# New RWKV states of the samples accumulated in PSUM in the layout of the outputs

## The chip, the cores and the metric

The kernel runs on one core of one Trainium2 chip. The metric is the device time of one execution in microseconds (us). Before the change the median of three runs is 1883.43 us (1877.42 to 1886.05). The profile is of one further execution, which took 1890.77 us; from its first to its last instruction it spans 1888.9 us.

## The reference, cut to what matters

The reference is one step of a two-layer decoder trunk: an even layer with MLA attention and RWKV-7 heads side by side, and an odd layer with gated linear attention and eight experts. Only the RWKV state of the even layer matters here:

```python
def rwkv7_scan(r, w, k, v, a, b, S0):
    def step(S, inp):
        rt, wt, kt, vt, at, bt = inp
        sa = jnp.einsum('bhvk,bhk->bhv', S, at)
        S = S * wt[:, :, None, :] + sa[..., None] * bt[:, :, None, :] + vt[..., None] * kt[:, :, None, :]
        return S, jnp.einsum('bhvk,bhk->bhv', S, rt)
```

A state S is a matrix [value, key] of 64 x 64 for each of the 8 heads. The prompt (256 tokens) starts from zero. The 8 samples of 8 tokens start from `state_rwkv` and hand back `new_rwkv_sample` of shape [sample, head, value, key], 1 MB in all. After a sample's 8 tokens, the new state is S0 decayed by the product of its eight w, plus the sum over the eight tokens of u b and v k, where u is the matrix product with the state (`sa`) and each b and k is decayed from its token to the end. All is fp32.

## The kernel before, in words

Every engine has its own program, written out by hand in blocks; the engines meet only in semaphores, and in a barrier at the end of a block. `next_part()` (L152) is two barriers with a clearing of semaphores between them. Nothing reorders the work: its order is the order of the lines.

The RWKV part lies between two calls of `next_part()` (L1150, L1779) and has three blocks.

**Block 1** makes r, w, k, v, a and b of all 320 tokens, with the channels on the partitions (four groups of 128 channels, two heads each). At its end the state S0 of each sample is turned by TensorE into S0T (key on the partitions, L1382, taken by ScalarE at L1321), and b and k are turned into rows with the tokens on the partitions: rowB and rowK, each of two tiles of 128 prompt tokens and one of the 64 sample tokens (L1393; taken in turn by VectorE, L1280, and ScalarE, L1325). rowV is made in the same way earlier (L1356, L1307). `wends` is the decay of each sample over its eight tokens (L1272).

**Block 2** inverts small triangular matrices per chunk of 64 tokens.

**Block 3** (L1494 to L1776) runs over the prompt's four chunks of 64 tokens. On TensorE `own_terms` and `transitions` make each chunk's terms, `step(c)` (L1560) carries the state on, `from_state(c)` (L1567) gives the outputs y. On VectorE `taken` takes the transitions (its last instruction, L1662, frees TensorE for the own terms of chunks 2 and 3), `advance(c)` (L1671, L1673) adds and decays the state, `y_add(c)` adds y. The samples' u comes at L1623 and is copied to U2. Their new states are made so: for each head VectorE spreads u and v over the samples (`spread`: ub and vb, L1683, L1684, each u or v times the 0/1 mask `bsel`), TensorE multiplies with the rows of b and of k (`new_states`, L1577, L1578: keys on the partitions, [sample, value] in 512 columns of one bank), VectorE adds S0T and multiplies with `wends` (`new_state`, L1689, L1690). Only two banks and two ub/vb buffers take turns. The result has keys on the partitions and the output wants values there: so TensorE turns the prompt's state and the eight samples' states (L1654, nine times four transposes), ScalarE and VectorE copy them in turn (L1767, L1741), and SP issues nine stores of 128 KB each (L1774, whose line in the profile is the helper's, L241). SP then waits for all of them, and block and part end.

The next part begins with four loads of 1 MB (L1895, `ring`) and with TensorE's L1918; none of it starts before the barrier. ScalarE's last work of block 3 ahead of the copies is `hT` (L1761, L1762), behind a wait for the y of all chunks.

Of the kernel before, what the change touches and what calls it, by code (L numbers as in the profile page):

```python
# [10 lines left out]
ALU = mybir.AluOpType  # L11
# [4 lines left out]
P = 128  # L16
# [42 lines left out]
def constants():  # L59
# [43 lines left out]
    bsel[:64] = (i[:64] // DS == np.arange(NB)[None, :])  # L103
# [36 lines left out]
def model(nc, A, O):  # L140
# [22 lines left out]
    with ctx:  # L163
# [243 lines left out]
        with ExitStack() as ev:  # L407
# [744 lines left out]
            with ExitStack() as rk:  # L1152
# [11 lines left out]
                with ExitStack() as st:  # L1164
# [12 lines left out]
                    rn = sbuf(st, "kk_norm", [P, 3, RH])  # L1177
                    rx = dif[:, :, :].rearrange("p c t -> p (c t)")[:, 0:3 * RDIM].rearrange("p (i h d) -> p i h d", i=3, h=RH)
# [3 lines left out]
                     kk_full, kk_var, kk_root, rn_ready, rx_ready, bc_full, kk_ready, ex_in, ex_out, bo_ready, bo_full, b_ready, k_ready, bonus_ready,  # L1182
# [3 lines left out]
                         "norm_full", "kk_ready", "exp_in", "exp_out", "bonus_in", "bonus_sum", "b_ready", "k_ready", "bonus_ready",  # L1186
                         "v_turned", "v_taken", "rows_turned", "rows_act", "rows_dve"))
                    kk, rT, kT, vT = t1, rwT[:, 0:4, :], rwT[:, 4:8, :], rwT[:, 8:12, :]
                    with nc.Block() as block:
# [14 lines left out]
                        def _(v):  # L1204
# [67 lines left out]
                            dv(v, v.tensor_copy(wends[:, :, :], bonus[:, :, SEQ + DS - 1:TOK:DS]))  # L1272
                            v.wait_ge(bo_full, 1)
# [3 lines left out]
                            for n in range(0, 6, 2):  # L1277
                                v.wait_ge(row_full, n + 1)
                                r = TILES[n % 3][1]
                                v.tensor_copy((rowB, rowK)[n // 3][0:r, n % 3, :], ps[n % 4][0:r, :]).then_inc(row_dve, 1)  # L1280
# [3 lines left out]
                        def _(s):  # L1284
# [37 lines left out]
                            for n in range(1, 6, 2):  # L1322
                                s.wait_ge(row_full, n + 1)
                                r = TILES[n % 3][1]
                                s.activation((rowB, rowK)[n // 3][0:r, n % 3, :], ps[n % 4][0:r, :], ACT.Copy).then_inc(row_act, 1)  # L1325

                        @block.tensor
                        def _(t):
# [25 lines left out]
                            for i, (lo, r) in enumerate(TILES):  # L1354
                                for c in range(4):
                                    mm = t.transpose(ps[5 + i][0:r, c * P:(c + 1) * P], vT[:, c, lo:lo + r], C("ident"))  # L1356
                                mm.then_inc(v_full, 1)
# [26 lines left out]
                            for n in range(6):  # L1384
                                lo, r = TILES[n % 3]
                                if n < 4:
                                    t.wait_ge(st_free, n + 5)
                                else:
                                    t.wait_ge(row_act if n % 2 else row_dve, n // 2 - 1)
                                for c in range(4):  # L1390
                                    if n % 3 == 0:
                                        t.wait_ge(b_ready if n < 3 else k_ready, c + 1)
                                    mm = t.transpose(ps[n % 4][0:r, c * P:(c + 1) * P], (bF, kF)[n // 3][:, c, lo:lo + r], C("ident"))  # L1393
# [96 lines left out]
                with ExitStack() as st:  # L1490
# [8 lines left out]
                    U2 = sbuf(st, "U2", [64, RDIM])  # L1499
                    ub = sbuf(st, "ub", [64, 2, NB, RD])  # L1500
                    vb = sbuf(st, "vb", [64, 2, NB, RD])
                    SN = S0T
                    NR = 8
                    OB = (4, 6, 2, 3)
                    srow2 = rwT[0:RD, :, :].rearrange("p c t -> p (c t)")[:, 0:NR * RDIM].rearrange("p (n k) -> p n k", n=NR)
                    yv = mixT[:, 4:8, :]
                    row_out = [Signal(sem(f"row_out{n}")) for n in range(NR)]
                    (a_full, a_ready, r_full, r_ready, w_full, wu_act, wu_dve, p_full, p_ready, q_full, q_dve, q_act, s_full, s_sum, s_ready,
                     y_full, y_added, sy_full, sy_ready, tr_full, mv_full, rhs_copied, r2_ready, u2_full, u2_ready, y2_full, y2_ready, blk_ready, n_full,
                     n_ready, o_full, o_act, o_dve) = (sem(x) for x in (  # L1510
                         "a_turned", "a_ready", "mv_first", "mv_ready", "w_full", "w_act", "w_dve", "p_full", "p_ready", "q_full", "q_dve", "q_act",
                         "s_full", "s_sum", "s_ready", "y_full", "y_added", "sy_full", "sy_ready", "sy_turned", "mv_full", "rhs_copied", "rhs2_ready", "u2_full",
                         "u2_ready", "y2_full", "y2_ready", "blk_ready", "new_full", "new_ready", "row_full", "row_act", "row_dve"))
# [11 lines left out]
                    with nc.Block() as block:  # L1525
                        @block.tensor
                        def _(t):
# [42 lines left out]
                            def new_states(hs_):  # L1570
                                for h in hs_:
                                    h0, pr = 64 * (h % 2), h // 2
                                    t.wait_ge(blk_ready, h + 1)
                                    if h % 2 == 0 and pr >= 2:
                                        t.wait_ge(n_ready, pr - 1)
                                    out = ps[pr % 2][h0:h0 + 64, :]
                                    t.matmul(out, rowB[0:64, 2, h * RD:(h + 1) * RD], ub[:, h % 2, :, :].rearrange("p b v -> p (b v)"), start=True, stop=False)  # L1577
# [1484 lines left out]
```

## Time and profile before

| | us |
|---|---|
| median of the runs | 1883.43 |
| profiled execution, and its span | 1890.77, 1888.9 |
| TensorE busy | 1790.3 |
| VectorE busy | 666.3 |
| ScalarE busy | 353.5 |
| mean granted clock, share of the full one | 0.962 |

The busy times are of the whole kernel, whose larger part is the experts' layer. The part that is changed is read from the timelines: a row of a timeline has the start, the length from the first start to the last end, engine, line, operation, output and inputs with their shapes, and the count; in brackets stands how long the engine sat idle before it and who let it go. Matmuls are shown with modelled ends, so that pitches are taken from starts. A plain fp32 matmul shows as two matmul records, a transpose as one.

### The profile page before, as it was taken

How to read it: one execution, taken by the hardware profiler on the slowest of the kernel's cores; microseconds unless marked ns; L12 is line 12 of the kernel's file. 1: busy time of each engine (PE TensorE's matmuls, PEld its weight loads, DVE VectorE, ACT ScalarE, POOL GpSimd, SP SyncE). 2: the span in 40 equal slices, each digit the busy share in tenths (PEclk: the TensorE clock that was granted, in tenths of full speed). 3: DMA queues.
4: the chain of work that ended last, by engine and by line, in shares of the span. 5: the costliest groups of instructions: out<-in, count | busy, mean ns of one | idle time of the engine just before them, and what ended most of it. 6: DMA issues, size and time to landing. Idle time of an engine off the chain costs nothing.

```text
span 1888.9 us, 42360 instructions
## 1 busy us (share of the span) xinstructions
PE 1790.3 (95%) x19238; PEld 1148.9 (61%) x19238; DVE 666.3 (35%) x1243; ACT 353.5 (19%) x584; POOL 29.7 (2%) x37
## 2 busy tenths in 40 slices
PE   7989898689799999998999999999999999999997
PEld 6957564587599999996833535344353443535344
DVE  4534332774675554656642110121102111120121
ACT  3223231501243332444310000000000000000002
POOL 0010000000000000000000000000000000000000
PEclk9989998698799999999989999999999999999998
DMA  9130540200654444425499999999999999997994
GB/s 289 45 109 1 150 142 11 37 3 2 181 155 142 150 145 126 155 68 150 143 379 416 417 412 417 397 382 417 364 417 373 405 409 366 417 354 290 399 416 159
DMA packets 166440, 463.28 MB, mean 245 GB/s; under 512 B 27770, under 2 KB 110876, under 8 KB 135412
## 3 DMA queue, kind: packets, MB, share of 16 engines
q1 hardware_dynamic: 164910, 457.37, 65.2%
q8 instruction: 151, 2.47, 0.5%
q0 software_dynamic: 1152, 3.15, 0.4%
q14 instruction: 29, 0.24, 0.0%
q10 hardware_dynamic: 198, 0.05, 0.0%
HBM read 451.57 MB, written 8.95 MB: 244 GB/s over the span
## 4 chain that ended last, share of the span: by engine, by line
PE 52%; DVE 1%; ACT 0%; issue 0%; DVEq 0%; ACTq 0%
PE bank L2623 46%; PE bank L2591 1%; PE bank L310 1%; PE bank L312 1%; PE bank L311 1%; PE bank L2554 0%; PE bank L2475 0%; PE bank L2597 0%; PE bank L2561 0%; PE bank L2490 0%; PE bank L2509 0%; PE bank L2482 0%; ACT ring L2787 0%; DVE mixT L2805 0%; PE bank L2494 0%; PE bank L2686 0%
## 5 line engine op out<-in xcount | busy, mean ns | idle before, releaser
L2623 PE MATMUL bank<-ring,x 128*32 128x512 f32 (+1 forms) x6144 | 587.5, 540 | 0.0
L2623 PEld LDWEIGHTS bank<-ring,x 128*32 128x32 f32 x6144 | 195.0, 110 | 359.9 <-issue 357.2
L2623 PE MATMUL bank<-ring,hid 128*32 128x256 f32 x5376 | 291.5, 379 | 0.0
L2623 PEld LDWEIGHTS bank<-ring,hid 128*32 128x32 f32 x5376 | 174.7, 110 | 117.1 <-issue 3.1
L310 PE MATMUL bank<-x_hi,w_hi 128*128 128x320 f32 (+1 forms) x488 | 151.8, 311 | 0.0
L312 PE MATMUL bank<-x_hi,w_lo 128*128 128x320 f32 (+1 forms) x488 | 150.8, 309 | 0.0
L311 PE MATMUL bank<-x_lo,w_hi 128*128 128x320 f32 (+1 forms) x488 | 150.8, 309 | 0.0
L2129 DVE TENSOR_TENSOR w_lo<-ring,w_hi 128x2048 fp32r<-128x2048 f32 (+2 forms) x51 | 112.5, 2208 | 96.2 <-ACT w_hi L2053 95.9
L2987 DVE TENSOR_TENSOR hrow<-sil,bank 128x512 f32<-128x512 f32 (+1 forms) x48 | 26.9, 616 | 296.1 <-PE bank L2623 296.1
L2950 DVE TENSOR_TENSOR xT<-xT,bank 128x320 f32<-128x320 f32 x56 | 23.5, 483 | 277.4 <-PE bank L2591 277.4
L2053 ACT ACTIVATE w_hi<-ring 128x2048 fp32r<-128x2048 f32 (+2 forms) x51 | 94.1, 1846 | 128.9 <-PE bank L312 124.3
L2769 ACT ACTIVATE sil<-bank 128x512 f32<-128x512 f32 (+1 forms) x48 | 22.6, 544 | 478.9 <-PE bank L2623 478.9
L310 PEld LDWEIGHTS bank<-x_hi,w_hi 128*128 128x128 f32 (+1 forms) x488 | 90.9, 186 | 1.9 <-issue 1.0
L311 PEld LDWEIGHTS bank<-x_lo,w_hi 128*128 128x128 f32 (+1 forms) x488 | 90.9, 186 | 0.6 <-issue 0.2
L312 PEld LDWEIGHTS bank<-x_hi,w_lo 128*128 128x128 f32 (+1 forms) x488 | 90.9, 186 | 0.4
L2776 ACT ACTIVATE Y<-bank 128x256 f32<-128x256 f32 x24 | 7.5, 384 | 403.8 <-PE bank L2623 403.8
L310 PE MATMUL bank<-hid,w_hi 128*128 128x320 f32 x240 | 75.2, 313 | 4.1 <-DVE w_lo L2129 4.1
L311 PE MATMUL bank<-hid,w_hi 128*128 128x320 f32 x240 | 74.8, 312 | 0.0
L312 PE MATMUL bank<-hid,w_lo 128*128 128x320 f32 x240 | 74.8, 312 | 0.0
L2969 DVE COPY listed<-bank 32x2 f32<-32x2 f32 x108 | 16.5, 153 | 145.9 <-PE bank L2597 144.5
L310 PE MATMUL bank<-proj_x_hi,proj_w_hi 128*128 128x320 f32 (+1 forms) x160 | 51.2, 320 | 6.5 <-DVE proj_w_lo L587 6.5
L311 PE MATMUL bank<-proj_x_lo,proj_w_hi 128*128 128x320 f32 (+1 forms) x160 | 50.5, 316 | 0.0
(569 smaller groups left out, 2209.7 us busy)
## 6 DMA issues: line engine op xcount, KB each, us to landing
ring<-in_moe_w_gu SPq DMA_DIRECT2D x128, 1024.0 KB, 15.9
ring<-in_moe_w_down SPq DMA_DIRECT2D x112, 1024.0 KB, 13.1
ring<-in_moe_w_gu SPq DMA_DIRECT2D x128, 768.0 KB, 10.7
ring<-in_ffn_w_gu_even SPq DMA_DIRECT2D x44, 512.0 KB, 4.9
pages<-in_cache_mla SPq DMA_DIRECT2D x128, 144.0 KB, 2.4
ring<-in_w_in_odd SPq DMA_DIRECT2D x12, 1024.0 KB, 5.6
ring<-in_ffn_w_down_even SPq DMA_DIRECT2D x10, 1024.0 KB, 5.1
proj_ring<-in_w_in_even SPq DMA_DIRECT2D x9, 1024.0 KB, 8.0
```

The source lines that it names most:

```text
L310: t.matmul(out, w_hi, x_hi, start=start, stop=False)
L311: t.matmul(out, w_hi, x_lo, start=False, stop=False)
L312: return t.matmul(out, w_lo, x_hi, start=False, stop=stop)
L2053: s.activation(whi[:, i % NSP, 0:size(i)], ring[:, i % NS, 0:size(i)], ACT.Copy).then_inc(hi_ready, 1)
L2129: v.tensor_tensor(wlo[:, i % NSP, 0:size(i)], ring[:, i % NS, 0:size(i)], whi[:, i % NSP, 0:size(i)].bitcast(F32), ALU.subtract).then_inc( ...
L2591: mm = t.matmul(ps[banks[y]][:, 0:TOK], Y[part, s_, z * P:(z + 1) * P], selT[part, s_, :], start=(s_ == 0), stop=(s_ == SG - 1), tile_posi ...
L2623: mm = t.matmul(ps[banks[g3]][SL * y:SL * y + SL, 0:w], act[:, g3, k, :], m_ring[:, slot, at + y * w:at + (y + 1) * w], start=start, stop= ...
L2769: ins = s.activation(sil[:, s_, 0:quarter(g)], ps[s_][:, 0:quarter(g)], ACT.Silu)
L2776: s.activation(Y[:, s_, :], ps[bank][:, 0:256], ACT.Copy).then_inc(y_ready, 1)
L2950: last = v.tensor_tensor(xT[:, 2 * y + z, :], xT[:, 2 * y + z, :], ps[bank][:, 0:TOK], ALU.add)
L2969: last = v.tensor_copy(listed[SL * y:SL * y + SL, s_, :], ps[6][SL * s_:SL * s_ + SL, 0:2])
L2987: ins = v.tensor_tensor(hrow[:, 512 * s_:512 * s_ + n], sil[:, s_, 0:n], ps[3 + s_][:, 0:n], ALU.mult)
```

## The change

It has these parts.

- Block 1, VectorE: eight small multiplications make `bks`, the samples' columns of b and of k times `wends` of their sample (each 128 x 64).
- Block 1, TensorE and the copies: the rows are five banks of 512 columns, no longer six: b and k of the two prompt tiles (banks 0 to 3), and bank 4 with the samples' decayed b in partitions 0 to 63 and their decayed k in partitions 64 to 127, by eight matmuls with the identity in two column tiles. rowB[:, 2] gets bank 4 whole. Bank 4 waits for `bonus_ready` and `bks_ready`. The samples' v is also written to partitions 64 to 127 (four matmuls with the identity, one more copy of ScalarE, to rowK).
- Block 3, VectorE: the mask `bsel` has 128 rows. `spread(h)` makes BKb, the rows of b and k of head h times the mask, one instruction of 128 x 512. Four stand at the block's start, four after the L1703 of before; between L1703 and these, four instructions of 128 x 512 multiply S0T with `wends` in place. U2 is written into rowK, below v.
- Block 3, TensorE: the new `new_states(pr)` has, for each sample and each of two heads, one matmul of the decayed S0T with the identity and one of [u; v] with BKb, accumulated at 64 partitions x 64 columns: 32 matmuls a pair of heads, values on the partitions, in four banks of their own. The order is step 2, from_state 2, states of pair 0, step 3, states of pair 1, from_state 3, pairs 2 and 3.
- The end: four copies of 128 x 512 (VectorE pairs 0 and 2, ScalarE 1 and 3, behind `hT`), four stores of 256 KB, and one turn, copy and store of 128 KB for the prompt. The 32 transposes of samples' states go, with their copies.

```diff
+                            v.wait_ge(k_ready, 4)
+                            for n, src in enumerate((bF, kF)):
+                                for c in range(4):
+                                    last = v.tensor_tensor(bks[:, n, c, :]..., src[:, c, SEQ:TOK]..., wends[:, c, :]...to_broadcast([P, NB, DS]), ALU.mult)
+                            last.then_inc(bks_ready, 1)
...
+                                if i == 2:
+                                    s.activation(rowK[64:128, 2, :], ps[7][64:128, :], ACT.Copy)
...
+                                    if i == 2:
+                                        t.matmul(ps[7][64:128, cols], vT[:, c, lo:lo + r], C("ident"), start=True, stop=True, tile_position=(0, 64))
...
+                                        for q in range(2):
+                                            mm = t.matmul(ps[4][64 * q:64 * q + 64, cols], bks[:, q, c, :], C("ident"), start=True, stop=True, tile_position=(0, 64 * q))
...
-                            def new_states(hs_):
-                                for h in hs_:
-                                    t.wait_ge(blk_ready, h + 1)
-                                    t.matmul(out, rowB[0:64, 2, h * RD:(h + 1) * RD], ub[:, h % 2, :, :]..., start=True, stop=False)
-                                    mm = t.matmul(out, rowK[0:64, 2, h * RD:(h + 1) * RD], vb[:, h % 2, :, :]..., start=False, stop=True)
+                            def new_states(pr):
+                                for b in range(NB):
+                                    for h in (2 * pr, 2 * pr + 1):
+                                        hs, _, _ = head(h)
+                                        t.matmul(ps[N_BANK[pr]][hs, b * RD:(b + 1) * RD], S0T[:, b, pr, :], C("ident")[:, hs], start=True, stop=False, tile_position=(0, hs.start))
+                                        mm = t.matmul(ps[N_BANK[pr]][hs, b * RD:(b + 1) * RD], UV2[:, h * RD:(h + 1) * RD], BKb[:, h, b, :], start=False, stop=True,
+                                                      tile_position=(0, hs.start))
+                                mm.then_inc(n_full, 1)
...
-                            for n in range(1 + NB):
-                                for pr in range(4):
-                                    src = ST[:, NCH, pr, :] if n == 0 else SN[:, n - 1, pr, :]
-                                    mm = t.transpose(ps[OB[n % 4]][0:RD, pr * P:(pr + 1) * P], src, C("ident"))
+                            for pr in range(4):
+                                mm = t.transpose(ps[5][0:RD, pr * P:(pr + 1) * P], ST[:, NCH, pr, :], C("ident"))
...
+                            for pr in range(4):
+                                last = v.tensor_tensor(S0T[:, :, pr, :], S0T[:, :, pr, :], wends[:, pr, :]...to_broadcast([P, NB, RD]), ALU.mult)
+                            last.then_inc(s0_ready, 1)
+                            for h in range(4, RH):
+                                last = spread(h)
+                            last.then_inc(blk_ready, 1)
...
+                            for pr in (1, 3):
+                                s.wait_ge(n_full, pr + 1)
+                                s.activation(news[:, pr, :, :]..., ps[N_BANK[pr]][:, :], ACT.Copy).then_inc(n_act, 1)
...
+                            for pr in range(4):
+                                sp.wait_ge(n_act if pr % 2 else n_dve, pr // 2 + 1)
+                                store(sp, O["new_rwkv_sample"][0, :, 2 * pr:2 * pr + 2].rearrange("b h v k -> (h v) b k"), news[:, pr, :, :])
+                            sp.wait_ge(o_act, 1)
+                            store(sp, O["new_rwkv_prompt"][0, 0].rearrange("h v k -> v h k"), srow2.rearrange("v (h k) -> v h k", h=RH))
```

## Rows read from the trace of the kernel before

**Rows 1.** The profile's page, part 1: busy time, share, instructions.

```profile
PE 1790.3 (95%) x19238; PEld 1148.9 (61%) x19238; DVE 666.3 (35%) x1243; ACT 353.5 (19%) x584; POOL 29.7 (2%) x37
```

**Rows 2.** Timeline of TensorE, the end of block 3 and the next part.

```profile
458.36 0.66 PE L1567 MATMUL bank<-hT,ST 64*64 64x64 f32 x16
...
480.73 5.92 PE L1654 MATMUL bank<-consts,S0T 128*64 128x128 f32 x32
492.85 4.61 PE L1918 MATMUL bank<-mixT,consts 128*128 128x320 f32 x8 [6.20 <-PEq L157]
```

**Rows 3.** Timeline of SP: the sample stores, and the next part's loads.

```profile
482.54 6.08 SPq L241 DMA_DIRECT2D out_new_rwkv_sample<-rwT  x8
492.80 5.34 SPq L1895 DMA_DIRECT2D ring<-in_w_out_even  x4
```

**Rows 4.** Stretches: length; busy of PE, PEld, DVE, ACT, POOL; granted clock, DMA share, GB/s.

```profile
335.00:345.00 10.00, 3.22 (x21) 2.90 (x21) 7.74 (x19) 6.35 (x13) 0.00 (x0) 0.50 0.94 146
430.00:440.00 10.00, 10.00 (x130) 10.00 (x129) 0.00 (x0) 1.18 (x2) 0.00 (x0) 0.54 0.01 2
460.00:465.00 5.00, 4.83 (x44) 2.05 (x42) 4.93 (x11) 1.82 (x4) 0.00 (x0) 1.00 0.02 5
470.00:475.00 5.00, 5.00 (x10) 1.25 (x8) 4.15 (x8) 0.00 (x0) 0.00 (x0) 0.50 0.00 0
482.00:483.00 1.00, 1.00 (x7) 0.84 (x5) 0.51 (x1) 0.32 (x1) 0.00 (x0) 0.50 0.08 13
490.00:491.00 1.00, 0.00 (x0) 0.00 (x0) 0.00 (x0) 0.00 (x0) 0.00 (x0) 0.50 0.65 95
```

**Rows 5.** Timeline of VectorE in block 1.

```profile
362.80 1.68 DVE L1257 TENSOR_TENSOR t<-t,bank 128x320 f32<-128x320 f32 x4
...
372.48 1.68 DVE L1275 TENSOR_TENSOR bonus<-bank,rwT 128x320 f32<-128x320 f32 x4
...
375.51 0.69 DVE L1280 COPY rowK<-bank 128x512 f32<-128x512 f32 x1 [0.16 <-PE bank L1393]
```

**Rows 6.** Timeline of ScalarE, the end of block 1.

```profile
375.95 0.59 ACT L1325 ACTIVATE rowK<-bank 64x512 f32<-64x512 f32 x1 [2.72 <-PE bank L1393]
```

**Rows 7.** Timeline of TensorE in block 1, and block 2's start.

```profile
355.16 2.82 PE L1356 MATMUL bank<-consts,rwT 128*128 128x128 f32 x12
...
376.84 1.56 PE L1419 MATMUL bank<-hT,bF 64*64 64x128 f32 x24 [0.93 <-PEq L1189]
```

**Rows 8.** Timeline of VectorE in block 3.

```profile
444.88 0.67 DVE L1703 TENSOR_TENSOR rhs<-rhs,bank 64x512 f32<-64x512 f32 x1
449.03 0.42 DVE L1705 TENSOR_TENSOR ST<-bank,wend 128x256 f32<-128x256 f32 x1 [3.48 <-PE bank L1553]
...
450.31 0.41 DVE L1662 TENSOR_TENSOR hT<-bank,hT 128x256 f32<-128x256 f32 x1
...
465.78 0.69 DVE L1690 TENSOR_TENSOR S0T<-S0T,wends 128x512 f32<-128x512 f32 x1
466.39 0.41 DVE L1677 TENSOR_TENSOR mixT<-mixT,bank 128x256 f32<-128x256 f32 x1
```

**Rows 9.** One line (L1623): min/median/max ns, first and last start.

```profile
L1623 PE MATMUL bank<-rhs,XT x16: 218/218/218, 450.5 to 451.4; 64*64 64x64 f32 x16
```

**Rows 10.** Timeline of TensorE, two matmul groups with 128 x 64 weights and 64 columns.

```profile
126.41 1.15 PE L828 MATMUL bank<-qpT,consts 128*64 128x64 f32 x16
...
329.17 1.15 PE L1066 MATMUL bank<-mixT,uv 128*64 128x64 f32 x32 [0.58 <-DVE mixT L1107]
```

**Rows 11.** Timeline of TensorE's weight loads where the tile shape changes.

```profile
441.70 0.36 PEld L1612 LDWEIGHTS bank<-consts,SY 128*64 128x64 f32 x4 [0.17 <-issue]
442.26 0.85 PEld L1606 LDWEIGHTS bank<-AV,XT 64*64 64x64 f32 x16 [0.20 <-issue]
```

**Rows 12.** Timeline of ScalarE in block 3.

```profile
463.18 1.92 ACT L1761 ACTIVATE hT<-bonus,vecs 128x320 f32<-128x320 f32 x4 [6.09 <-PE bank L1567]
465.00 1.25 ACT L1762 ACTIVATE hT<-gT 128x1280 f32<-128x1280 f32 x1
```

More of the change, by code:

```diff
@@ L1276, in _ @@
                             last.then_inc(bonus_ready, 1)
-                            for n in range(0, 6, 2):
+                            for n in (0, 2, 4):
                                 v.wait_ge(row_full, n + 1)
-                                r = TILES[n % 3][1]
-                                v.tensor_copy((rowB, rowK)[n // 3][0:r, n % 3, :], ps[n % 4][0:r, :]).then_inc(row_dve, 1)
+                                v.tensor_copy(ROWS[n], ps[n][:, :]).then_inc(row_dve, 1)
                             v.wait_ge(bonus_ready, 1)
@@ L1383, in _ @@
                                 mm.then_inc(st_full, 1)
[L1384 to L1389, printed above, removed]
[L1390 to L1393 removed]
+                            for n in range(5):
+                                t.wait_ge(*((st_free, n + 5) if n < 4 else (bonus_ready, 1)))
+                                if n == 4:
+                                    t.wait_ge(bks_ready, 1)
+                                for c in range(4):
+                                    cols = slice(c * P, (c + 1) * P)
+                                    if n < 4:
+                                        src, lo = (bF, kF)[n // 2], TILES[n % 2][0]
+                                        if n % 2 == 0:
+                                            t.wait_ge(b_ready if n < 2 else k_ready, c + 1)
+                                        mm = t.transpose(ps[n][:, cols], src[:, c, lo:lo + P], C("ident"))
+                                    else:
+                                        for q in range(2):
+                                            mm = t.matmul(ps[4][64 * q:64 * q + 64, cols], bks[:, q, c, :], C("ident"), start=True, stop=True, tile_position=(0, 64 * q))
                                 mm.then_inc(row_full, 1)
@@ L1568, in from_state @@
                                 mm.then_inc(y_full, 1)
-                            def new_states(hs_):
-                                for h in hs_:
-                                    h0, pr = 64 * (h % 2), h // 2
-                                    t.wait_ge(blk_ready, h + 1)
[L1574 to L1577, printed above, removed]
-                                    mm = t.matmul(out, rowK[0:64, 2, h * RD:(h + 1) * RD], vb[:, h % 2, :, :].rearrange("p b v -> p (b v)"), start=False, stop=True)
-                                    mm.then_inc(n_full, 1)
+                            def new_states(pr):
[6 more added lines that the diff above has]
+                                mm.then_inc(n_full, 1)
                             for i in range(2):
```

109 lines of the change are left out of this document (44 added, 65 removed).

## The prediction

> **What bounds the kernel now.** I read the page first: TensorE is busy for 95% of the span [rows 1], but the change touches one stage of some 120 us, so the share says little and the stage has to be read by itself. Then the timelines of its engines from 355 to 500 us, and the stretches with clock and DMA share. The reader is to see three things. First, the part ends in a tail that no other work covers: the transposes of the samples' states start at 480.73 and last 5.92 us [rows 2], the eight sample stores are issued from 482.54 to 488.62 [rows 3], and TensorE then stands still until 492.85, where "PEq L157" says that it was the barrier of the part that held it [rows 2]. Nothing of the next part starts earlier, not even its loads (SP, 492.80 [rows 3]). So whatever moves this barrier moves the whole rest of the kernel by as much. Second, the tail ends with the DMA engines and not with SP: their share is 0.08 in 482 to 483 and 0.65 in 490 to 491 [rows 4], with full slices between; I read 7.7 us of all engines for nine stores of 128 KB, which is 0.85 us a store, against a pitch of 0.68 at which SP issued them. Packets begin at about 482.9 and end at about 490.65, and from there to TensorE's restart are 2.2 us. Third, ahead of the tail the new states are a chain of VectorE and TensorE in turn, and TensorE's clock is lost in it: granted 1.00 (2.4 GHz) in 460 to 465, 0.50 (1.2 GHz) in 470 to 475, where ten matmul records of 512 columns fill 5 us [rows 4].
>
> **Block 1, what is added and what goes.** At its end VectorE gets eight products of 128 x 64. The trace has none of that size; by VectorE's rows of 256 and 512 columns (pitches 0.33 and 0.61 us, the second from the starts 465.78 and 466.39 [rows 8]) a column costs 1.1 ns over a base of 0.06 us, so 64 columns come to 0.13 us and eight to 1.0 us. They stand ahead of L1275, which ran from 372.48 for 1.68 us [rows 5] and now ends near 375.2. The first two copies of rows follow to 376.4. Bank 4 needs `bonus_ready`, at 375.2: eight matmuls with 128 columns, 16 records over two column tiles, 0.9 us if the tiles overlap, 1.7 us if not or at half the clock. Its copy starts at about 376.5 and ends at 377.2. Before, the last to end was ScalarE at 375.95 + 0.59 = 376.54 [rows 6], with VectorE's at 376.20 [rows 5], and TensorE's next block began at 376.84 [rows 7]. So block 1 ends 0.7 us later (0.3 to 1.6).
>
> Further ahead, four matmuls for the second v are eight records of 128 columns behind the twelve of L1356, which took 2.82 us, 0.22 us each [rows 7]: at most 1.8 us for TensorE, and one copy of 0.6 us for ScalarE, behind which stand its copy of the norms, the exponentials and the copies of g. What covers it is VectorE: it is busy without a gap and takes the first result of this chain at 362.80 [rows 5], and by my reading of ScalarE's timeline the exponentials come 3 us ahead of their use. The cover is just enough for the norm, with some tenths left; I count 0, and 1.2 us at worst.
>
> **Block 3, the eight new products on VectorE.** The first four (128 x 512, pitch 0.61, 2.4 us) stand in front of two copies whose readers come ten microseconds later; VectorE was idle there. Cost nothing. The other eight (four decays, four spreads) go between L1703, over at 445.5, and L1705, which started at 449.03 after 3.48 us of idleness [rows 8]. 8 x 0.61 = 4.9 us, so that L1705 starts at 450.4, 1.3 us late. Who waits for that: TensorE's own terms of chunks 2 and 3 stand behind L1662, which ended at 450.72 [rows 8]; one wait of 0.18 us ahead of it goes, so it ends at 451.8. But TensorE was busy with L1623 until its last start at 451.4 [rows 9]. The delay that gets through is 0.4 us.
>
> **Block 3, the chain of states.** From there everything is 0.4 us late until from_state(2), whose 16 records started at 458.36 [rows 2]: it now ends near 459.4. Before, VectorE did four spreads ahead of advance(2), which then started at 460.77; these go, and advance(2) runs at 459.0, as soon as step(2) is done. Now the new matmuls: 128 x 64 weights, 64 columns, 32 to a pair of heads. Two rows bound them. L1066 has just this shape with its column tiles taken in turn: 32 records (16 matmuls) in 1.15 us, less the 0.22 us length of the last, a pitch of 30 ns a record, 60 ns a matmul. L828 has the same shape and stays in one column tile: 16 records in 1.15 us, 62 ns a record, 124 ns a matmul [rows 10]. The new order is two matmuls in one tile, then two in the other, which lies nearer to the first. I take 60 ns: 32 x 60 = 1.9 us a pair (4.0 at the other end). So, with d for a pair and a change of tile shape (64 x 64 to 128 x 64 or back) at 0.2 us as between L1606 and L1612 [rows 11], five of them in all: pair 0 from 459.4 to 461.3, step(3) to 462.2, pair 1 to 464.2, from_state(3) to 465.1, pairs 2 and 3 to 469.0. In letters, from_state(3) ends at 461.3 + 2d and the last pair at 461.4 + 4d.
>
> The Trainium skill ("TensorEngine Tiling (Array Packing)", section Tiling Modes) says that a change of tiling mode, unlike a change of tile, drains TensorE. That speaks against this order, which puts three blocks of one mode between blocks of the other. The trace agrees as to the sign, with 0.17 and 0.20 us of idle weight loads; the rule gives no other price.
>
> **The end.** ScalarE stands behind from_state(3) with `hT`, 463.18 to 466.25, 3.1 us [rows 12], and copies pair 1 after it: 465.1 + 3.1 + 0.7, so that the second sample store is issued at 469.0. (The first, of pair 0, leaves at about 464 and is out of the way.) Pair 3 is copied at 469.8, the prompt's state at 470.5. SP needs 1.33 us to issue a load of 1 MB cut into 1024 pieces (four in 5.34 us) and 0.65 to 0.76 for a store of 512 pieces [rows 3]; a new store has 1024 pieces of 256 B, so I take 1.33: issues at 469.0, 470.3, 471.7 and 473.0. The pieces are as long as before, so that the DMA engines need for the three of 256 KB and the one of 128 KB 7 x 0.85 = 6.0 us. Begun 1.2 us after the issue, they end at 476.2, later than the last issue by enough. Plus the 2.2 us of the barrier: TensorE restarts at 478.4 and not at 492.85. In letters, 474.6 + 2d by this road and 468.2 + 4d by way of the last pair, which takes over above d = 3.2 us.
>
> **The sum.** 492.85 - 478.4 = 14.4 us won, 0.7 us lost in block 1: 13.7 us. The last 0.2 I give for the order within a pair, which is not quite L1066's. 13.5 us off the profiled execution is 1890.8 - 13.5 = 1877.3 us. That execution is 7.3 us over the median of the runs, which is noise and no part of the change; against the median the forecast is 1883.4 - 13.5 = 1869.9 us. All that stands after the barrier, the experts above all, is as before.
>
> **Rivals.**
>
> A. The tiles don't overlap, or the clock stays at 1.2 GHz (either gives about 120 ns a matmul). For it: in the old chain the clock fell [rows 4], and in 430 to 440 it was 0.54 although TensorE was busy all the time, with matmuls of 16 columns [rows 4]. Against it: the old chain was full of gaps, which the new lacks, and 460 to 465, with the 64-column matmuls of step(3) and from_state(3) in it, had 1.00 [rows 4]. d = 4.0: restart at 484.2, won 8.7, less 0.7: 8.0 us, 1875.4 us.
>
> B. The stores from 128 partitions go faster than those from 64. The loads of 1 MB, which have 1 KB pieces, show that the engines can do more. Then SP's issues bound: last issue 473.0 + 1.3 + 0.4 + 2.2 = 476.9, and the win is 15.2 us: 1868.2 us. Against it: in 335 to 345, mostly the loads of the old states in pieces of 256 B, the share was 0.94 at 146 GB/s [rows 4], the stores' rate.
>
> C. Block 1 gives more back: the second v goes through with 1.2 us and bank 4 with 1.6, both at 1.2 GHz. Win 11.5 us, 1871.9 us.
>
> D, the other side: both halves of A together, 240 ns a matmul, d = 7.7 us. The restart is at 468.2 + 30.8 = 499.0 plus 0.7, 6.9 us late: 1890.3 us, slower. It decides from d = 6.0 us, 187 ns a matmul. For it speaks only that both halves have a row; against it what was said under A, and that the tile order isn't that of L828.
>
> E. What VectorE now does ahead of L1705 holds more than one reader, or the new waits (s0_ready, blk_ready) come last: they are posted at 450.4, nine microseconds ahead of their use. I give this no time of its own.
>
> **Chances.** Forecast, between 12 and 15 us won: 0.58. A 0.16, B 0.08, C 0.12, D 0.03, none of these 0.03. A measurement of this kernel can tell about 0.5%, 9.4 us, from no change. The forecast and B lie beyond that, C mostly, A just inside; with the spread of the runs that gives 0.75 for faster, 0.21 for the same, 0.04 for slower. The range for 8 in 10 goes from 1864 (B and 4 us of spread) to 1878 us (A and some spread).
>
> **What would show it.** Right: no L1654 for the samples; records of the new matmuls at 30 ns pitch, a pair in 1.9 us; granted clock near 1.00 in 460 to 470 of the old count; L1705 some 1.3 us later, the own terms 0.4; the DMA share full for about 6 us, and L1918 at about 479, counted from the same start. Block 2's first matmul at 377.5. Wrong: pairs of 4 us with starts 60 ns apart, a clock at 0.50 there, a DMA tail that is longer than 7 x 0.85 us, or a restart that is set by something other than the store of the last states. The forecast falls if L1918 comes after 484, or if the time behind it differs by more than 2 us.

## The result and the profile after

The changed kernel takes 1874.28 us (median of 20 runs, 1863.34 to 1884.31), the kernel before 1886.65 us (20 runs, 1876.17 to 1893.05). The ratio is 0.9933, 95% interval 0.9917 to 0.9950: by the ratio 12.6 us faster, from 9.4 to 15.7 us (the two medians differ by 12.4). Forecast were 13.5 us. The profiled execution of the changed kernel spans 1871.8 us, 17.1 less than that of before, and not all of this is the change.

The page's part 1, which answers to [rows 1]: some 200 more records on TensorE, and yet 13 us less busy, part of it clock.

```profile
PE 1777.3 (95%) x19446; PEld 1151.1 (61%) x19446; DVE 658.1 (35%) x1237; ACT 352.1 (19%) x582; POOL 29.6 (2%) x37
```

TensorE's timeline in block 3, which answers to [rows 2]:

```profile
447.73 0.27 PE L1561 MATMUL bank<-WU,rowB 64*64 64x64 f32 x2
...
462.37 0.66 PE L1579 MATMUL bank<-hT,ST 64*64 64x64 f32 x16
462.96 0.34 PE L1586 MATMUL bank<-consts,S0T 128*64 128x64 f32 x4
...
464.76 0.33 PE L1587 MATMUL bank<-BKb,rowK 128*64 128x64 f32 x4
465.02 0.68 PE L1572 MATMUL bank<-ST,PT 64*64 64x64 f32 x16
465.63 0.34 PE L1586 MATMUL bank<-consts,S0T 128*64 128x64 f32 x4
...
468.31 0.34 PE L1586 MATMUL bank<-consts,S0T 128*64 128x64 f32 x4
...
472.24 0.62 PE L1663 MATMUL bank<-consts,ST 128*64 128x128 f32 x4
479.54 1.94 PE L1915 MATMUL bank<-mixT,consts 128*128 128x320 f32 x3 [6.67 <-PEq L157]
```

The first row is the start of the own terms of chunks 0 and 1, which I use as the zero of the stage. In the kernel before it is this row:

```profile
444.06 0.27 PE L1549 MATMUL bank<-WU,rowB 64*64 64x64 f32 x2
```

So the next part began 48.8 us behind the zero before [rows 2], and begins 31.8 us behind it now. The samples' turns are gone; the four pairs of heads lie around step(3) and from_state(3), pairs 2 and 3 from 468.31 to 472.24, 3.9 us for 128 records in all, 64 matmuls.

ScalarE and SP at the end, which answer to [rows 12] and [rows 3]:

```profile
468.43 1.92 ACT L1758 ACTIVATE hT<-bonus,vecs 128x320 f32<-128x320 f32 x4 [7.32 <-PE bank L1579]
470.25 1.26 ACT L1759 ACTIVATE hT<-gT 128x1280 f32<-128x1280 f32 x1
471.42 0.57 ACT L1762 ACTIVATE rwT<-bank 128x512 f32<-128x512 f32 x1
472.35 0.60 ACT L1762 ACTIVATE rwT<-bank 128x512 f32<-128x512 f32 x1 [0.36 <-PE bank L1587]
```

```profile
467.59 6.22 SPq L237 DMA_DIRECT2D out_new_rwkv_sample<-rwT  x4
473.86 1.17 SPq L237 DMA_DIRECT2D out_new_rwkv_prompt<-rwT  x1
```

The stretches, which answer to [rows 4] (the clock is the third number from the end, then DMA share and GB/s):

```profile
468.00:473.00 5.00, 4.86 (x146) 4.46 (x141) 1.44 (x3) 4.22 (x8) 0.00 (x0) 1.00 0.29 57
...
474.00:475.00 1.00, 0.00 (x0) 0.00 (x0) 0.00 (x0) 0.00 (x0) 0.00 (x0) 1.00 1.05 212
...
477.00:478.00 1.00, 0.00 (x0) 0.00 (x0) 0.00 (x0) 0.00 (x0) 0.00 (x0) 0.50 0.38 57
```

The reader is to see that pair 1's copy (471.42) stands behind `hT`, that the clock stays at 1.00 through all pairs, and that the DMA engines move 212 GB/s in the tail, where they moved some 152 before (nine stores of 128 KB in 7.8 us).

VectorE and TensorE at the end of block 1, which answer to [rows 5] and [rows 7]:

```profile
377.10 0.63 DVE L1278 TENSOR_TENSOR sample_bk<-bF,wends 128x64 f32<-128x64 f32 x4
377.65 0.63 DVE L1278 TENSOR_TENSOR sample_bk<-kF,wends 128x64 f32<-128x64 f32 x4
378.19 1.68 DVE L1283 TENSOR_TENSOR bonus<-bank,rwT 128x320 f32<-128x320 f32 x4
...
381.07 0.69 DVE L1287 COPY rowB<-bank 128x512 f32<-128x512 f32 x1
```

```profile
379.93 1.09 PE L1408 MATMUL bank<-consts,sample_bk 128*64 128x128 f32 x16 [1.80 <-DVE bonus L1283]
382.09 2.20 PE L1434 MATMUL bank<-hT,bF 64*64 64x128 f32 x36 [1.07 <-PEq L1191]
```

And VectorE in block 3, which answers to [rows 8]:

```profile
448.56 0.67 DVE L1707 TENSOR_TENSOR rhs<-rhs,bank 64x512 f32<-64x512 f32 x1
449.15 2.48 DVE L1709 TENSOR_TENSOR S0T<-S0T,wends 128x512 f32<-128x512 f32 x4
451.56 2.48 DVE L1688 TENSOR_TENSOR BKb<-rowB,consts 128x512 f32<-128x512 f32 x4
453.97 0.41 DVE L1715 TENSOR_TENSOR ST<-bank,wend 128x256 f32<-128x256 f32 x1
```

### The profile page after: what moved, and what is told of

The parts are those of the page before. It is cut to its first block, busy times and chain, and to the rows that moved or that the text cites. A ratio compares the mean times of both kernels' runs of the same rounds, so it can differ in the third digit from the quotient of the medians.

```text
span 1871.8 us, 42760 instructions
## 1 busy us (share of the span) xinstructions
PE 1777.3 (95%) x19446; PEld 1151.1 (61%) x19446; DVE 658.1 (35%) x1237; ACT 352.1 (19%) x582; POOL 29.6 (2%) x37
## 4 chain that ended last, share of the span: by engine, by line
PE 52%; ACT 1%; DVE 0%; issue 0%; DVEq 0%; ACTq 0%
PE bank L2620 47%; PE bank L2588 1%; PE bank L310 1%; PE bank L312 1%; PE bank L311 1%; PE bank L2472 1%; PE bank L2594 0%; PE bank L2558 0%; PE bank L2551 0%; PE bank L2487 0%; PE bank L2479 0%; ACT ring L2784 0%; PE bank L2491 0%; ACT ring L2783 0%; PE bank L2683 0%; ACT mix_hi L2702 0%
## 5 line engine op out<-in xcount | busy, mean ns | idle before, releaser
L2966 DVE COPY listed<-bank 32x2 f32<-32x2 f32 x108 | 16.5, 153 | 145.7 <-PE bank L2594 144.3
## 6 DMA issues: line engine op xcount, KB each, us to landing
ring<-in_moe_w_down SPq DMA_DIRECT2D x112, 1024.0 KB, 14.4
```

The source lines that it names most:

```text
L2966: last = v.tensor_copy(listed[SL * y:SL * y + SL, s_, :], ps[6][SL * s_:SL * s_ + SL, 0:2])
```

## The experiments

An execution of this kernel can't be told from another by less than some microseconds, so most experiments are read by pieces of one profile, taken between the starts of two records. "Block 1" is from kk_norm on VectorE (L1234 of before) to block 2's first matmul, "y" from block 3's first matmul to the own terms, "tail piece" from the own terms to the next part's first matmul. All are in us.

```
                    block 1     y    tail piece
before                 28.4   18.8     48.8
before, again          28.4   17.3     48.6
after                  29.0   17.3     31.8
after, again           31.1   18.8     31.8
e1 one tile, then      29.0   17.3     36.7
e6 old chain           28.4   17.3     41.9
e2 halves              31.0   18.8     32.7
e3 old places          31.0   18.8     32.7
e8 upper half          29.0   17.3     33.4
e9 lower half          31.0   18.8     33.6
e7 v later             29.0   17.3     31.8
e10 v later, again     30.2   18.8     31.8
e5 all changes         29.0   18.8     29.8
e11 all, again         29.1   18.8     29.8
```

**Both kernels once more (c0_before, c1_after).** No edit.

> The kernel before, profiled a second time, to tell what of the 17.1 us between the two profiled spans is the change. Measured is the piece from the first record of own_terms (L1549) to the next part's first matmul (L1918): 48.9 us in the first profile. Theory: this piece is steady (within 1 us), and the other differences between the profiles (4.7 us ahead of block 1's end, 2.7 us in the 16-column matmuls of the samples' y, 3.8 us behind the barrier) are TensorE's clock in one execution and the next. Rival: the change altered those too, then they stay as in the first profile of before.

> The changed kernel, profiled a second time. Piece from the first record of own_terms (L1561) to L1915: 31.8 us in the first profile, expected within 1 us. From the first record of block 3 (L1592) to own_terms: 17.3 us in the first profile against 18.7 before; if that is the clock it moves by one or two us again, if it is the change it stays.

The tail piece came back within 0.2 us in both (48.79 and 48.64, 31.80 and 31.81): 16.8 to 17.0 us are the change. The y piece has two values, 17.3 and 18.8, and both kernels show both. What was wrong is that I held the first part to be steady: block 1 is 28.4 in both profiles of before (and in e6, which has the old block 1), but 29.0 or 31.1 in the changed kernel. The second profile of the changed kernel shows where, VectorE and then TensorE:

```profile
364.62 2.20 DVE L1259 TENSOR_TENSOR t<-t,bank 128x320 f32<-128x320 f32 x4 [0.51 <-PE bank L1379]
```

```profile
356.39 1.97 PE L1367 MATMUL bank<-consts,rwT 128*128 128x128 f32 x8
...
377.66 1.98 PE L1408 MATMUL bank<-consts,sample_bk 128*64 128x128 f32 x16 [2.56 <-DVE bonus L1283]
380.70 3.58 PE L1434 MATMUL bank<-hT,bF 64*64 64x128 f32 x64 [1.06 <-PEq L1191]
```

Eight transposes of v took 1.97 us where the first profile's took 1.09: the granted clock was 0.50 (1.2 GHz) from 356 to 360, while in the first profile it had risen by then. TensorE came out of v and g late: VectorE sat idle for 0.51 us ahead of L1259 (L1257 of before), whose four instructions then took 2.20 us, with waits between them, in place of 1.68 [rows 5]. Bank 4's sixteen records took 1.98 us in place of 1.09. Of the 2.1 us between the two profiles, 1.2 are there when VectorE starts L1283 (25.1 us behind kk_norm in the first, 353.10 to 378.19; 26.3 in the second, 349.64 to 375.92), and 0.9 come from bank 4 on. The other profiles divide in the same way: e2, e3 and e9 have v and bank 4 at 1.97 to 1.98 and block 1 at 31.0, e1 and e8 have 1.09 at both and 29.0. The kernel before has v at 1.2 GHz in all its profiles (2.82 us for twelve in the first [rows 7]) and there loses nothing by it: the cover was enough for its own matmuls, and not for eight records more.

**One column tile after the other (e1_serial).**

```diff
-                                for b in range(NB):
-                                    for h in (2 * pr, 2 * pr + 1):
+                                for h in (2 * pr, 2 * pr + 1):
+                                    for b in range(NB):
```

> Changed kernel, but within a pair of heads all 16 matmuls of the first head (one column tile) come ahead of the 16 of the second. Theory (the win needs the two column tiles side by side): 117 to 124 ns a matmul and 3.8 to 4.0 us a pair, against 58 ns and 1.9 us; the last pair then sets the end, and the piece from own_terms to L1915 grows from 31.8 by about 6.5 us to 38. Rival (the pace is the issue of records, whatever the tile): 58 ns and 31.8 us as before.

```profile
463.12 0.33 PE L1586 MATMUL bank<-consts,S0T 128*64 128x64 f32 x2
463.29 0.28 PE L1587 MATMUL bank<-BKb,rowK 128*64 128x64 f32 x2
463.41 0.28 PE L1586 MATMUL bank<-consts,S0T 128*64 128x64 f32 x2
...
466.61 0.28 PE L1587 MATMUL bank<-BKb,rowK 128*64 128x64 f32 x2
466.82 0.68 PE L1572 MATMUL bank<-ST,PT 64*64 64x64 f32 x16
```

A matmul (two records) begins every 117 ns, a pair takes 3.7 us in place of 2.06 from its start to step(3), and the tail piece grows by 4.9 us. The rival is out: it is the two tiles side by side that make the pair short. 6.5 us were expected. The last pair does come 6.4 us later (30.9 us behind the zero for 24.5), but less is left to store behind it: the last packet follows it by 3.7 us, and by 5.2 in the changed kernel, where stores still stood in the queue. The expectation had let the whole delay through.

**The old chain without the old end (e6_noturns).** The chain of new states as before; the samples' states leave unturned in four stores of 256 KB from S0T, so 32 transposes, eight copies and the eight small stores are left out.

```diff
-                            for n in range(1 + NB):
-                                sp.wait_ge(o_dve if n % 2 else o_act, n // 2 + 1)
-                                ...
+                            for pr in range(4):
+                                sp.wait_ge(n_ready, pr + 1)
+                                store(sp, O["new_rwkv_sample"][0, :, 2 * pr:2 * pr + 2].rearrange("b h v k -> (h v) b k"), SN[:, :, pr, :])
```

> The kernel before with its chain of new states as it was, but the samples' states are stored straight from S0T in four stores of 256 KB, so that 32 transposes, eight copies and eight stores of 128 KB are left out (the stored states are not turned). It tells the tail from the chain. Theory: the tail is worth about 7 of the 17 us and the chain about 10: piece from own_terms to the next part 42 us, total 6 to 7 us below the kernel before. Rival (the end is set by the DMA engines alone, and the chain hides behind them): piece near 33, nearly all of the win.

Tail piece 41.9, as the theory had it; total 0.9961 of the kernel before (0.9933 to 0.9989). So of the 17.0 us, 6.9 are the turns and the queue of small stores behind them, and 10.1 are the chain. The split is that of this kernel: its tail ends with the prompt's state, which is turned behind the whole chain, and whose last packet comes 1.9 us behind the last one of the samples. The chain still loses the clock in this kernel, as in [rows 4]:

```profile
460.00:465.00 5.00, 5.00 (x9) 1.43 (x10) 4.13 (x8) 0.00 (x0) 0.00 (x0) 0.50 0.24 52
```

**What sets the rate of the stores (e2_halves, e3_oldplaces, e8_upper, e9_lower).** The forecast had 0.85 us for 128 KB, and the changed kernel showed 0.61 to 0.64. e2 cuts each store in two; e3 also writes to the places of before (the states land elsewhere); e8 and e9 read the same half of the partitions for both stores (half of the states are another head's).

```diff
-                                store(sp, O["new_rwkv_sample"][0, :, 2 * pr:2 * pr + 2].rearrange("b h v k -> (h v) b k"), news[:, pr, :, :])
+                                for a in range(2):
+                                    store(sp, O["new_rwkv_sample"][0, :, 2 * pr + a].rearrange("b v k -> v b k"), news[64 * a:64 * a + 64, pr, :, :])
...
+                                    store(sp, O["new_rwkv_sample"][0, 2 * pr + a].rearrange("h v k -> v h k"), news[64 * a:64 * a + 64, pr, :, :])
```

> Changed kernel, each sample store of 256 KB from 128 partitions cut into two of 128 KB from 64 partitions; the same pieces of 256 B go to the same places. In the changed kernel the DMA engines moved 215 GB/s in this tail (0.61 to 0.64 us for 128 KB), before the change 155 (0.85 us). Theory (the number of source partitions sets the rate): back to about 155 GB/s and 0.85 us for 128 KB, and the piece from own_terms to the next part grows from 31.8 to about 33.5 us. Rival (the order of places in memory, or the smaller number of DMAs, did it): 215 GB/s stays, 31.8 to 32.3 us.

> As e2 (64 partitions, 128 KB a store), but each store writes one sample's eight heads, pieces of a partition 16 KB apart as before the change and no longer 128 KB (the states land in the wrong heads). Theory of the partitions: same rate as e2, about 155 GB/s. Rival (places): slower than e2, and e2 stays at 215 GB/s.

> As e2, but both 64-partition stores of a pair read partitions 64 to 127 (half of the states are the other head's). In e2 the first store of each pair, from partitions 0 to 63, ran at about 153 GB/s and the second, from 64 to 127, at about 245. Theory (the half of the partitions decides): all eight at 240 or more, 0.53 us for 128 KB, the prompt's store still at 150; piece from own_terms to the next part 31.7 us against 32.7. Rival (the second of two stores is the faster, or the head's place in memory decides): rates alternate as in e2 and the piece stays at 32.7.

> As e8_upper with partitions 0 to 63 for both. Theory: all at about 153 GB/s, 0.84 us for 128 KB, as in the kernel before; piece 33.7 us. Rival: rates alternate as in e2, 32.7 us.

The rates in 40 slices of the tail (window 467 to 478 in the changed kernel, 473 to 478.5 in e2, 457 to 472 in e8, 466 to 481 in e9, 455 to 477 in e6), one fence for each kernel in this order:

```profile
GB/s 0 0 0 0 0 71 222 218 217 210 16 0 0 0 60 0 0 0 0 0 0 61 224 192 241 217 211 206 213 235 209 217 212 225 191 206 179 99 0 0
```

```profile
GB/s 0 34 153 149 156 153 140 117 224 276 209 140 130 231 261 186 141 119 242 253 201 138 117 244 268 182 145 125 239 255 173 151 108 224 277 201 155 136 23 0
```

```profile
GB/s 110 44 0 0 0 0 0 14 153 152 165 154 158 154 156 154 154 154 154 156 135 142 266 27 0 0 0 0 0 0 0 63 126 227 374 377 344 382 382 366
```

```profile
GB/s 0 0 0 0 44 0 0 0 0 0 67 153 154 163 150 56 0 0 0 0 0 0 114 155 161 154 160 153 152 155 155 154 156 156 154 156 153 145 15 0
```

```profile
GB/s 0 0 0 0 0 209 218 50 0 0 0 0 1 216 217 42 0 0 0 0 0 2 216 218 41 0 0 0 1 215 219 42 4 148 87 0 0 0 0 0
```

Neither of my first two theories stood as written. e2 gave neither 155 nor 215 GB/s, but 120 to 155 and 240 to 280 by turns. I took that for slow stores from the lower half and fast stores from the upper, and e8 and e9 put that out: upper half alone 154, lower half alone 154, tail pieces 33.4 and 33.6 against 31.8 with whole stores. The reading was wrong from the start. e2's fence has seven stores (six of the samples and the prompt's) in 5.1 us, and its rate rises six times, every 0.7 us, which is the pitch at which SP issues them. So it isn't every second store that is fast: the rate is at 150 at the start of the first store and at the end of the last, and it rises once between each store and the next. A store alone needs 0.85 us for its 128 KB, so neighbours overlap. The overlap of two stores from different halves is the likely place of the 240 to 280; the trace doesn't tell which packet belongs to which store. e8 and e9 fit: stores from the same half follow each other at an even 154, and the one rise, 266, comes in e8 where the prompt's store, from the lower half, follows those from the upper. On average e2 moves 180 GB/s. The places in memory do nothing (32.7 in e3 as in e2).

What stands: with pieces of 256 B, stores from one half of the partitions give 154 GB/s, whichever half; stores from 128 partitions give 205 over the whole tail of the changed kernel and 212 to 219 in their middle, and e6's four, each alone in the queue, show the same 215 to 219. Which part of the path saturates at one half isn't shown by these runs.

**The second v later (e7_vlater, e10_vlater_again).** The four matmuls go to bank 1, behind ScalarE's copy of it, where TensorE waits for `bonus_ready`.

```diff
-                                    if i == 2:
-                                        t.matmul(ps[7][64:128, cols], vT[:, c, lo:lo + r], C("ident"), start=True, stop=True, tile_position=(0, 64))
...
+                                if n == 4:
+                                    t.wait_ge(row_act, 1)
+                                    for c in range(4):
+                                        mm = t.matmul(ps[1][64:128, c * P:(c + 1) * P], vT[:, c, SEQ:TOK], C("ident"), start=True, stop=True, tile_position=(0, 64))
+                                    mm.then_inc(v_full, 1)
```

> Changed kernel, only the second copy of v is made later: its four matmuls go to bank 1 behind ScalarE's copy of the rows, where TensorE waits for bonus_ready, and ScalarE copies it there. Block 1 from kk_norm (VectorE) to block 2's first matmul took 28.4 us before the change, 29.0 in two profiles of the changed kernel and 31.1 in the third, whose clock was still 1.2 GHz at the second v. Theory (the second v is on the path when the clock is low, and bank 4's matmuls at a low clock are the rest): 28.9 to 29.0 us whatever the clock does there. Rival (the 31.1 came from somewhere else): it can be 31 again.

> e7 once more, for its block 1 in another phase of the clock. In the changed kernel and its variants block 1 (kk_norm to block 2) took 29.0 to 29.1 us in the profiles where the v matmuls had got 2.4 GHz, and 31.0 to 31.1 in those where they still ran at 1.2. Theory: with v later at most 29.7 us in either phase. Rival: 31 if the clock is low there. If the clock is high again the run says nothing.

Both had 1.2 GHz at the transposes of v, and in both the cure works: L1259 runs for 1.67 us without a wait. The first, TensorE and then VectorE:

```profile
360.27 2.82 PE L1365 MATMUL bank<-consts,rwT 128*128 128x128 f32 x12
...
374.20 1.09 PE L1408 MATMUL bank<-consts,bF 128*128 128x128 f32 x8
375.13 1.04 PE L1408 MATMUL bank<-consts,kF 128*128 128x128 f32 x8
```

```profile
367.91 1.67 DVE L1259 TENSOR_TENSOR t<-t,bank 128x320 f32<-128x320 f32 x4
```

Its block 1 took 29.0, where the changed kernel with 1.2 GHz at v took 31.0 or 31.1. But e7's clock had risen by the turns of b and k, and bank 4 ran at 2.4 GHz too (16 records in 1.09 us), so that the 2.0 us are the two causes together. What the cure gives by itself is read at L1283: it starts 25.2 us behind kk_norm in both, as in the first profile, and not 26.3. e10's block 1 took 30.2, not at most 29.7; its TensorE:

```profile
368.60 3.67 PE L1391 MATMUL bank<-consts,srow 64*128 64x64 f32 x32
372.20 1.97 PE L1408 MATMUL bank<-consts,bF 128*128 128x128 f32 x8
373.96 1.91 PE L1408 MATMUL bank<-consts,kF 128*128 128x128 f32 x8
375.81 1.30 PE L1397 MATMUL bank<-consts,rwT 128*64 128x128 f32 x5
```

Here the rows of b and k were turned at 1.2 GHz (1.97 and 1.91 us for e7's 1.09 and 1.04), and the later v stands behind them and ahead of bank 4. So the expectation failed by 0.5 us, and e7's "whatever the clock does" with it: the wait at L1259 is settled, and the rest of block 1's loss goes with the clock in another place.

**The version that the readings point to (e5_best, e11_best_again).** ScalarE copies pair 1 ahead of `hT`; the prompt's state is turned ahead of pairs 2 and 3, copied by VectorE and stored third; v later; three spreads behind the copy of U2.

```diff
                             from_state(3)
-                            new_states(2)
-                            new_states(3)
                             t.wait_ge(s_ready, NCH)
                             t.wait_ge(y2_ready, 1)
...
                             mm.then_inc(o_full, 1)
+                            new_states(2)
+                            new_states(3)
...
+                            s.wait_ge(n_full, 2)
+                            s.activation(news[:, 1, :, :]..., ps[N_BANK[1]][:, :], ACT.Copy).then_inc(n_act, 1)
                             s.wait_ge(y_full, NCH - 1)
```

> The version that the readings point to. ScalarE copies pair 1 ahead of its hT; the second v is made later as in e7; the prompt's state is turned ahead of pairs 2 and 3, copied by VectorE and stored third; three of the four late spreads stand behind the copy of U2, where VectorE was idle for 3.6 us. Theory (the tail is what is left of the queue of stores when the last pair is there): last is the store of pair 3 alone, two units of 128 KB in place of seven; piece from own_terms to the next part about 30.1 us in place of 31.8, block 1 at 28.9; total 1.5 to 3 us below the changed kernel, some 15 us below the kernel before (ratio 0.992). Rival (TensorE's changes of tile shape and the later spreads cost what the order wins): 31.5 us or more, ratio 0.993.

> e5_best once more, timed again against the kernel before to narrow the interval, and profiled once more. Piece from own_terms to the next part 29.8 us again, block 1 at most 29.7 us in either phase of the clock; ratio 0.992 again, between 0.990 and 0.994.

Tail piece 29.8 in both profiles (30.1 expected), block 1 29.0 and 29.1. The second had 1.2 GHz at v (2.82 us for the twelve) and yet 29.1, like e7: in both the clock had risen by bank 4, so e10's case was not met again. SP in the first one:

```profile
467.94 1.23 SPq L237 DMA_DIRECT2D out_new_rwkv_sample<-rwT  x2
470.14 0.64 SPq L237 DMA_DIRECT2D out_new_rwkv_prompt<-rwT  x1
472.17 2.08 SPq L237 DMA_DIRECT2D out_new_rwkv_sample<-rwT  x2
```

Only the store of the last pair is issued behind the last copy. The ratio to the kernel before is 0.9916 (0.9885 to 0.9946) in one set of runs and 0.9892 (0.9861 to 0.9923) in the next, just outside the 0.990 to 0.994 that were expected there. It beats the kernel before clearly. That it beats the changed kernel (0.9933, 0.9917 to 0.9950) rests on the 2.0 us of the tail piece; the two were not timed side by side, and the intervals overlap. Which of the moves brought the 2.0 us was not taken apart.

## Why the prediction was right

The mechanism is the forecast one: the work ahead of a bare barrier got shorter, and the next part came earlier by as much. That the number was met has some luck in it. Two rivals with small chances came true as well, with opposite signs: B (0.08) in every profile with whole stores, C (0.12) in some.

**The tail is bare.** It held: whatever the barrier gained, the next part began earlier by. Read from the own terms (444.06 and 447.73), the next part was forecast at 34.3 us and came at 31.8.

**The eight products on VectorE.** L1705 was forecast 1.3 us late, of which 0.4 us gets through. Measured from the zero it was at 4.97 and is at 6.24, 1.3 us late; from_state(2) was at 14.30 and is at 14.64, 0.3 us late.

**The pairs.** 60 ns a matmul by L1066 [rows 10], measured 59 (from 468.31 to 472.24, less 0.15 us to the first transpose, are 3.78 us for the 64 matmuls of pairs 2 and 3), against 117 in one tile (e1). The granted clock was 1.00 throughout, so that rival A was off on both counts, and D with it. Five changes of tile shape were counted at 0.2 us each; before step(3) the last new record starts at about 464.87 and the next at 465.02, 0.15 us where the pitch is 0.03, and the way back is the same: 0.12 us each, 0.6 in all. The rule from the Trainium skill ("TensorEngine Tiling (Array Packing)", section Tiling Modes), that a change of mode drains the array, has the sign right; the price is small.

**The end: the term that was mis-sized.** The step "the DMA engines need for the three of 256 KB and the one of 128 KB 7 x 0.85 = 6.0 us" measured 4.5 us (from 472.9 to 477.4), because stores from 128 partitions go faster; that was rival B. Its argument against, that the old states' loads ran at 146 GB/s, was no evidence: those loads too touch 64 partitions only. The other 1.0 us are the issue of the second store, 24.3 us behind the zero for 24.9, first packets 0.9 us behind the issue and not 1.2, and 2.1 us from the last packet to the next part for 2.2. SP's issue of a store with 1024 pieces, taken as 1.33 us, was 0.39 to 0.74 us, and decided nothing. The 1.33 was a mean over four loads whose issues took 0.42, 0.58, 1.35 and 2.85 us: it rose with what was queued ahead. The prompt's store shows the same, with 512 pieces in 1.17 us behind the others, for 0.64 before the change. The 0.68 us between SP's issues before the change is also that of the last four alone; over all eight sample stores it was 0.78, still under the 0.85 us that the DMA engines needed, so that the reading stands.

**Block 1: right in one phase of the clock.** 0.7 us was forecast (0.3 to 1.6), and 0.5 came in the profiles with 2.4 GHz at v and bank 4 (28.44 to 28.98 us), 2.6 in those with 1.2 at both (31.06). The second is rival C almost to the tenth: it had 1.2 us for v and 1.6 for bank 4, 2.8 in all, and the four profiles with 1.2 GHz show 2.5 to 2.6. The cover "with some tenths left" was gone with the clock. C was given 0.12, and came in four of the seven profiles whose block 1 is that of the changed kernel.

**The sum.** By pieces the change is worth 17.0 us less 0.5 or 2.6, so 16.5 or 14.4, where 13.7 were forecast: the tail's surplus and block 1's loss went opposite ways. The timed runs say 12.6, from 9.4 to 15.7. The smaller of the two sums lies in the interval, the greater just outside it. The pieces between also move: in all seven profiles 31 us in block 1 go with 18.8 in the y piece and 29.0 with 17.3, while the kernel before has 28.4 with either. Taken whole, from kk_norm to the next part, the kernel before took 144.4 and 142.8 us in its two profiles and the changed one 126.4 and 130.4, so that the difference is anything from 12.4 to 18.0. Which mixture of phases the timed runs had is not known, and stays open; so does whether the change shifts the clock elsewhere.

**A sign that was badly chosen.** By the prediction's own words it falls if the time behind L1918 differs by more than 2 us. It does: 1396.1 us from there to the end before the change, 1392.3 after it. But the kernel before has 1391.6 in its second profile, and the changed one 1393.6 in its second. The sign told one execution from the next and not one kernel from the other, and by the same measure nothing shows that the change touches what stands behind the barrier.

**What else moves.** That the clock does move in places which the change doesn't touch is seen in a part of the MLA heads, the kernel before first and then e6, with the same code there:

```profile
136.00:144.00 8.00, 7.31 (x23) 4.87 (x23) 2.80 (x9) 1.40 (x5) 0.00 (x0) 0.50 0.00 0
```

```profile
136.00:144.00 8.00, 7.56 (x45) 5.58 (x45) 4.20 (x15) 2.80 (x10) 0.00 (x0) 1.00 0.01 2
```

By the end of that part (162 us) e6 is 7.8 us ahead of the kernel before, which is more than half of what the whole change brings. So the nearness of 12.6 to 13.5 is in part luck, and the evidence for the mechanism is the pieces.

## What to carry to other kernels

At a barrier, ask what the last store waits for and what is queued ahead of it: here ScalarE's 3 us of unrelated work stood in front of a copy, and moving it behind the copy, together with the earlier turn of the prompt's state, was worth 2.0 us more. A result that TensorE can accumulate in the layout of the output saves the turn, and its stores can read all 128 partitions in place of 64; but count what that puts into earlier blocks, and price TensorE's part there at 1.2 GHz as well, since cover of some tenths is no cover. Small differences are read from a piece between two records, in two profiles of each kernel, and not from the span.

## What the runs showed of the hardware

- Stores in pieces of 256 B: 154 GB/s from 64 partitions, lower or upper half alike (e8, e9); 205 to 219 GB/s from 128 partitions (the changed kernel, e6); stores from the two halves in turn, queued, 180 on average, with 120 to 155 and 240 to 280 by turns (e2). Where the pieces land (16 or 128 KB apart) made no difference (e3).
- fp32 matmuls with 128 x 64 weights and 64 columns: 59 ns each when two column tiles change every two matmuls, 117 ns when they change every sixteen.
- A change between 64 x 64 and 128 x 64 tiles cost 0.12 us over the pitch.
- A product of 128 x 64 on VectorE has a pitch of 0.135 us (eight from 377.10 to 378.19), 0.13 expected from rows of 256 and 512 columns.
